# Plain float32 products in place of three float32r products on split operands

## What is computed

```python
h = rmsnorm(x, ln_mix_g)
proj = h @ w_in                                   # split into dq, dk, dv, nq, ..., ng, mg
y_diff = diff_attention(dq, dk, dv, lam, ...)
y_nsa = nsa_attention(nq, k_cmp, v_cmp, k_slc, v_slc, k_win, v_win, sigmoid(ng))
mixed = merge0 * (y_diff @ w_proj_diff) + merge1 * (y_nsa @ w_proj_nsa)
x = x + mixed @ w_out
x = x + square(relu(rmsnorm(x, ln_mlp_g) @ w_mlp_up)) @ w_mlp_down
q, k, v, f_logit, gate = split(rmsnorm(x, norm_a_g_2) @ w_in_a_2)
x = x + (fox_attention(q, k, v, log_sigmoid(f_logit + b)) * silu(gate)) @ w_out_a_2
k, v = split(rmsnorm(x, kv_norm_g_2) @ w_kv_2)
q, gate = split(rmsnorm(x, norm_b_g_2) @ w_in_b_2)
x = x + (swa_sink_attention(q, k, v, sinks) * silu(gate)) @ w_out_b_2
```

## Time and profile before

| | |
|---|---|
| median of 3 runs | 2090.55 us |
| lowest, highest | 2073.0, 2091.24 us |
| span of the profiled execution, first to last instruction | 2072.2 us |
| PE busy | 1907.3 us (92%), 8846 matmuls |
| DVE, ACT, POOL busy | 908.2, 717.1, 368.5 us |
| granted TensorE clock, mean | 0.920 |

### The profile page before, as it was taken

One profiled execution on the slowest core, in us unless ns is written; L12 is line 12 of the kernel. 1 busy time (PEld: TensorE's weight loads), 2 busy tenths in 40 slices (PEclk: granted clock), 3 DMA queues, 4 the chain that ended last, 5 costly groups with the idle time before them and its releaser, 6 DMA issues.

```text
span 2072.2 us, 24116 instructions
## 1 busy us (share of the span) xinstructions
PE 1907.3 (92%) x8846; PEld 1443.5 (70%) x8846; DVE 908.2 (44%) x1569; ACT 717.1 (35%) x1525; POOL 368.5 (18%) x490
## 2 busy tenths in 40 slices
PE   3999898999979999898999999989999998798988
PEld 2888567877755655687788888777775556686647
DVE  2583364225534555334443243234623443453662
ACT  3223365122144555423342142233223442333550
POOL 4240132102114444111000000000102330020330
PEclk9999797999977999999899999989996878898889
DMA  5223121332101221322222332312221102132212
GB/s 138 73 91 127 46 66 56 102 102 81 41 24 38 52 51 40 123 95 93 72 87 101 102 102 83 101 63 80 89 85 46 47 21 82 61 102 65 52 26 81
DMA packets 148050, 154.85 MB, mean 75 GB/s; under 512 B 48973, under 2 KB 90173, under 8 KB 147961
## 3 DMA queue, kind: packets, MB, share of 16 engines
q1 hardware_dynamic: 141768, 152.74, 23.2%
q0 software_dynamic: 992, 0.86, 0.3%
q10 hardware_dynamic: 5200, 0.02, 0.3%
HBM read 123.15 MB, written 2.15 MB: 60 GB/s over the span
## 4 chain that ended last, share of the span: by engine, by line
PE 90%; DVE 4%; ACT 3%; ACTq 1%; issue 1%; POOL 0%; DVEq 0%; POOLq 0%
PE ps L1421 58%; PE ps L1650 11%; PE ps L1677 5%; PE ps L1697 4%; PE ps L1711 3%; PE ps L1658 2%; ACTq L476 1%; PE ps L1654 1%; PE ps L1692 1%; DVE qkt L1008 1%; PE ps L1549 1%; PE ps L1519 1%; PE ps L1620 1%; ACT qkt L633 1%; PE ps L1537 1%
## 5 line engine op out<-in xcount | busy, mean ns | idle before, releaser
L1421 PE MATMUL ps<-spl,ht 128*128 128x512 f32 x2496 | 581.3, 395 | 31.0 <-DVE spl L787 15.8
L1421 PEld LDWEIGHTS ps<-spl,ht 128*128 128x128 f32 x2496 | 476.5, 191 | 135.3 <-issue 14.8
L787 DVE TENSOR_TENSOR spl<-raw,spl 128x1024 fp32r<-128x1024 f32 x196 | 253.4, 1336 | 566.2 <-ACT spl L494 566.2
L494 ACT ACTIVATE spl<-raw 128x1024 fp32r<-128x1024 f32 x196 | 196.2, 1052 | 637.3 <-PE ps L1421 636.5
L1421 PE MATMUL ps<-ht,spl 128*128 128x512 f32 x1536 | 349.9, 390 | 2.0 <-DVE spl L787 2.0
L1421 PEld LDWEIGHTS ps<-ht,spl 128*128 128x128 f32 x1536 | 288.5, 188 | 62.7 <-issue 2.9
L1650 PE MATMUL ps<-qkt 64*128 64x256 f32 (+2 forms) x960 | 255.4, 378 | 11.3 <-issue 5.8
L978 DVE TENSOR_REDUCE nm<-ps 128x1 f32<-128x512 f32 (+5 forms) x320 | 150.7, 471 | 146.8 <-PE ps L1658 144.0
L614 ACT ACTIVATE pb<-ps,nm 128x512 f32<-128x512 f32 (+5 forms) x320 | 162.1, 511 | 119.0 <-DVE nm L978 118.7
L1650 PEld LDWEIGHTS ps<-qkt 64*128 64x128 f32 x960 | 160.5, 212 | 61.0 <-issue 42.6
L1421 PE MATMUL ps<-spl,uu 128*128 128x512 f32 x768 | 174.4, 389 | 0.0
(11 more groups left out here) (244 smaller groups left out, 1547.3 us busy)
## 6 DMA issues: line engine op xcount, KB each, us to landing
raw<-w_in SPq DMA_DIRECT2D x30, 1024.0 KB, 5.2
raw<-w_mlp_up SPq DMA_DIRECT2D x16, 1024.0 KB, 5.2
raw<-w_mlp_down SPq DMA_DIRECT2D x16, 1024.0 KB, 5.0
raw<-w_in_a SPq DMA_DIRECT2D x16, 1024.0 KB, 5.3
stq<-qkv SPq DMA_DIRECT2D x56, 256.0 KB, 2.7
raw<-w_in_b SPq DMA_DIRECT2D x8, 1024.0 KB, 4.9
stq<-qkv SPq DMA_DIRECT2D x48, 128.0 KB, 2.5
raw<-w_proj_diff SPq DMA_DIRECT2D x4, 1024.0 KB, 5.2
```

Source lines behind the costliest of these rows:

```text
L494: act.activation(SPL[:, n % 2, HI, 2 * k:2 * k + 2], RAW[:, n % 2, 2 * k:2 * k + 2], ACT.Copy).then_inc(hi_done, 1)
L787: dve.tensor_tensor(SPL[:, n % 2, LO, 2 * k:2 * k + 2], RAW[:, n % 2, 2 * k:2 * k + 2], SPL[:, n % 2, HI, 2 * k:2 * k + 2].bitcast(F32), A ...
L1421: last = pe.matmul(PS[:, b0 + b], left[:, x], right[:, y], start=(kt == 0 and i == 0), stop=(kt == UK * g["units"] - 1 and i == 2))
```

## The change

Each product becomes one matmul on float32 operands, and no half is made. The weight is multiplied straight from RAW, which now has four slots; SP refills a slot when PE has used it. HT, UU and QKT hold float32 values once, YS is Y itself, and a second copy of HT with the other norm's gains (HTK) feeds the key and value projection of the banded attention. ACT evicts the even slices of a norm and DVE the odd ones. ACT copies the queries and DVE the keys. The scores of both maps of a tile stand next to each other, followed by both masks. The reload of X now waits until PE has used the last unit that reads Y.

```diff
-        RAW = region("raw", "raw", [2, UK, W])
-        SPL = region("spl", "spl", [2, 2, UK, W], F32R)
+        RAW = region("raw", "raw", [SLOTS, UK, W])
...
-                    if n >= 2:
-                        sp.wait_ge(lo_done, 2 * (n - 1))
+                    if n >= SLOTS:
+                        sp.wait_ge(unit_used, n - SLOTS + 1)
...
-            weights(RUNS["merge"], skip=2, only=4)
-            sp.wait_ge(y_hi, 2 * KT)
-            sp.wait_ge(y_lo, 2 * KT)
+            weights(RUNS["merge"], skip=2, only=8)
+            sp.wait_ge(unit_used, RUNS["merge"][4]["unit"])
             sp.dma_start(X[:], I["x"][0].rearrange("(t p) n -> p t n", p=P)).then_inc(x_in[0], 16)
-            weights(RUNS["merge"], skip=4)
+            weights(RUNS["merge"], skip=8)
...
-            def split_hi(n, hold=()):
...
-                for k in range(2):
-                    act.activation(SPL[:, n % 2, HI, 2 * k:2 * k + 2], RAW[:, n % 2, 2 * k:2 * k + 2],
-                                   ACT.Copy).then_inc(hi_done, 1)
...
-                for kt in range(KT):
+                for kt in range(KT) if k == 3 else range(0, KT, 2):
                     act.wait_ge(x_tr, KT * k + kt + 1)
-                    act.activation(HT[:, HI, kt], PS[:, bank_of(k, kt)], ACT.Copy,
-                                   scale=1.0 if k == 3 else LNG[:, k, kt:kt + 1]).then_inc(x_hi, 1)
+                    act.activation(HT[:, kt], PS[:, bank_of(k, kt)], ACT.Copy,
+                                   scale=LNG[:, 4 if k == 3 else k, kt:kt + 1]).then_inc(x_even, 1)
...
-                for i, (x, y) in enumerate(((HI, HI), (HI, LO), (LO, HI))):
-                    last = pe.matmul(PS[:, b0 + b], left[:, x], right[:, y], start=(kt == 0 and i == 0),
-                                     stop=(kt == UK * g["units"] - 1 and i == 2))
-                return last
+                w = RAW[:, (g["unit"] + u) % SLOTS, k]
+                left, right = (src[:, kt, cols], w) if g["kind"] == "tok" else (w[:, cols], src[:, kt])
+                return pe.matmul(PS[:, b0 + b], left, right, start=(kt == 0), stop=(kt == UK * g["units"] - 1))
...
-                        for i, (x, y) in enumerate(((HI, HI), (HI, LO), (LO, HI))):
-                            pe.matmul(bank[:, 0:w], QKT[r, m.slot, 0, x, P * t:P * t + P],
-                                      QKT[r, m.slot, 1, y, P * a.first_key(t):P * t + P],
-                                      start=(i == 0), stop=False, skip_group_check=True)
+                        pe.matmul(bank[:, 0:w], QKT[r, m.slot, 0, P * t:P * t + P],
+                                  QKT[r, m.slot, 1, P * a.first_key(t):P * t + P],
+                                  start=True, stop=False, skip_group_check=True)
+                    for h in range(2):
+                        bank = PS[:, 2 * (idx % 2) + h]
                         if a.is_fox:
```

## The result

The changed kernel takes 2186.99 us (2185.85 to 2188.04, 4 runs) against 2081.78 before (2071.62 to 2091.24, 4 runs): 1.05 times the time, 95% interval 1.0443 to 1.0557. The profiled execution has a span of 2185.8 us, 113.6 more than before, where the sum of the prediction had 191. The kernel before varies by some 20 us from run to run here, the changed one by 2 us.

The account below looks back on a forecast made before the run. PE's busy time was taken as the bound. From 2072.2 us: +309 weight products, +3 narrow gates, -80 scores, -56 waits gone, +15 new wait gave 2264; 9 for longer runs made 2273 us, range 2218 to 2362.

Parts of the forecast that it names:

- +309: Weight products: 1728 products at 0.859 us plain instead of 0.680 add 309 us (+299 to +346).
- The bound of 0.880: Weight products: upper bound in us per plain product, if each half carries the 13 ns a float32r matmul takes over 512 cycles.
- rival 4: Weight products: four passes at float32r's price, 0.907 us a product, giving 2356 us; 5%.
- The three norms: Between PE's last product before a norm and its next: 8 us instead of 17.6, -10 each, -30 together.
- The new wait for X: Before w_out: PE stands 12 us while X reloads ahead of w_out's first unit; with the clock's fall, +15 us.
- PE's start: Kernel start: PE needs four slices, two made by DVE, instead of waiting for eight LO slices and half a weight; -5 us.
- the scores' term: Attention scores: plain maps side by side and fewer copies save 106 us, three quarters kept, -80; bounds -106 and 0.
- the copies: Attention: one copy by ACT and one by DVE replace four dependent instructions; perhaps 8 of 15.9 us of waits go.
- Rival 2: Attention scores: the two maps don't overlap, a pair takes as long as before, time 2353 us; 7%.
- Rival 3: Attention: it falls to the low clock, time at most 2544 us; 6%.
- Rivals 1 and 5: Plain matmuls: 1, they cost what float32r ones do, 1572 us, 3%; 5, weight products at low clock, 3740 us, 3%.
- Rival 6: Waits, chiefly at norms: they don't shrink because DVE and ACT are late in their new order, 2329 us; 6%.

Follow-up runs that it names:

- e5: Kernel before with only the weight products plain: one float32 matmul on the HI halves for three float32r ones, LO halves unused; 2388.07 us.
- e4: Changed kernel with the reload of X behind the first two units of w_out on SP instead of ahead of them; 2177.37 us.
- e1: Kernel before with the changed kernel's attention alone: plain scores of both maps side by side, masks after, weights still three float32r matmuls; 1930.49 us.
- e3: Kernel before with the changed kernel's plain scores and single copies, but each map's mask directly behind its own scores, so maps are apart; 2083.91 us.
- e6: Changed kernel with each map's mask behind its own scores, so the two maps' products no longer stand next to each other; 2356.14 us.
- e9: Kernel before with only the masks moved: map 0's three float32r score matmuls, map 1's three, then both masks; 1957.43 us.
- e2: Kernel before with the three float32r score matmuls of the two maps alternating and both masks following; 1948.9 us.
- e7: Kernel before with one float32r score matmul (HI by HI) per map in place of three, maps still apart; 1973.96 us.
- e10: Kernel before with one float32r score matmul (HI by HI) per map in place of three, maps next to each other, masks behind them; 1919.64 us.

## Why the prediction was wrong

**Right.** PE's time per product decided, and the halves' removal was worth only the waits. A plain product took 858.4 ns for 859 forecast, the mean of one matmul 592 to 599 ns for "near 600"; at the measured rate the term is +308 for +309, and e5, with the narrow gates left as they were, is 314 us of span above the kernel before (293 above its median). The bound of 0.880 and the four-pass price of 0.907 (rival 4) are off. The Trainium skill's sentence of four passes ("FP8 and Floating Point Precision", on TensorE's precision notes) fits only as two matmuls at two cycles a column, without float32r's 13 ns per pass (858.4 ns are 2060 cycles of 2.4 GHz, 4.02 a column). The three norms take 6.2, 7.6 and 7.5 us where 17.6, 16.6 and 17.6 were, -31 for -30. The new wait for X was 10.5 us for 12, and e4 shows its cause as it was given; taken out it gave 9.6 back, where the sum had +15 for it. PE's start moved by 2.2 us (43.73 to 41.52) for 5. Everything outside the four attentions grew by 277 us, where these terms make 285.5: the stages of weights and norms were right to 9 us.

**The step that failed** is the scores' term: "Other engines take some of it back ... That leaves three quarters, -80 us". Attention and its entries gave 163 us where -80 and about 15 of the waits were written. The direction and the mechanism, two maps side by side on PE, were right; the size was off by 68 us. Three parts of it were wrong.

1. Nothing was taken back. NSA's unit went from 13.22 us (756.70 to 769.92 before) to 10.26 (731.92 to 742.18), or 10.34 over ten units. I had 2.2 us of saving per unit and discounted it to 1.7; it was 2.9. DVE, at 107.52 of 177 us, had room, as its 122.61 of 228 already said. No row gave the size of the quarter taken off, and it cost the sum 26 us.
2. The pair was priced a little high. Side by side the second mask adds next to nothing: 0.21 us for both against the 0.32 that I kept; and the 256-wide tile, taken as 0.39 less, went from 1.34 to 0.76 us in the unit that follows 731.92. The four pairs of a unit save 2.7 us for the 2.2 forecast.
3. The clock was held fixed. I divided the saving by the clocks of before, so that a slow FOX stayed slow at 0.72. In fact the time at the low clock fell from 204 to 66 us, and FOX rose from 0.72 to 0.86, NSA from 0.93 to 0.99. e1 and e3 show that this comes with the overlap (83 against 192 us with the same plain matmuls), e5 that the weights do not bring it, and the middle of FOX that the clock goes with the overlap in all seven traces named there.

How much falls to each can be estimated from a unit's length at full clock, taken from the start times of its scores:

| | unit before, us | unit now, us | units | saved by units, us | saved by the stretch, us |
|---|---|---|---|---|---|
| DIFF | 11.83 | 9.25 | 8 | 21 | 25 |
| NSA | 13.22 | 10.34 | 16 | 46 | 57 |
| FOX | 15.15 | 12.58 | 8 | 21 | 48 |
| SWA | 11.86 | 9.71 | 8 | 17 | 33 |

That is 105 us by shorter units, for the 84 forecast at full clock, and 58 us by the clock and by entries and ends, for some 37 (14 by the division by the clocks, 8 by the copies, 15 of the waits). So of the 68 us some 26 are the discount, 21 the units and 21 the rest, most of it in FOX, where the larger part of the saving is the clock's. It is an estimate: no run changed the clock alone.

The time of 2273 has 9 us more, for runs like the two longer ones of the kernel before; the changed kernel has no such run in four.

**The rivals.** Rival 2 (no overlap) was priced at 2353 us; e6 is that kernel and took 2356. That it is so close is in part luck: the 2353 hold the 9 us for longer runs, and the pair took 2.43 us, not the 2.09 of before. In spans it is 2343 against 2354.3. Even so, the sum's other terms hold together, and it was the overlap's worth, 168 us for the 80 that I gave it, which put the result out of range. Rival 3 foresaw that attention's clock would move, and had the direction wrong: "the same rows are at work in less time", said against it, fits what the middle of FOX shows. Rivals 1 and 5 did not occur. Rival 6 didn't either; the norms' waits shrank as forecast.

The range failed with the term: its lower bound gave the scores at most 106 us, as though -106 excluded any more, although the trace of before showed FOX at a clock of 0.72, and the earlier trace rows gave no reason why it should stay there. With -106 in the sum the forecast would have been 2247 us, still 60 above what was measured.

## What to carry to other kernels

Where two products use different halves of the array's rows, put them next to each other with no full-row matmul between; look at the start times of such pairs in the trace before anything else is done to them. Here the masks' place between two score maps was worth 156 us of span between e1 and e3, and 117 to 142 on the old halves (e9, against the span and against the run beside it), more than the number format of the scores did in either order (e3 is within the spread of the kernel before, e1 18 us below e2). When a change makes matmuls run side by side, price the clock as a term of its own, with the low-clock stretches of before as its bound, rather than dividing by the clock that was. Don't take a discount off a sum of rows without a row that shows who would take it back. And judge "one matmul for three" by what one of them takes: plain float32 was dearer by 26% here, so it paid only in attention, where it shortened a chain of copies.

## What the runs showed of the hardware

- A plain float32 matmul of 512 columns appears as two matmuls of 429.2 ns each (439.48 us for 1024), a float32r one as one of 226.7 ns (348.22 us for 1536).
- Matmuls on the row halves 0 to 63 and 64 to 127, into different banks, ran side by side in both formats, even with all of the first half's matmuls ahead of the second's in the program (e9: six of 512 columns in 0.90 us). The Trainium skill, "TensorEngine Tiling (Array Packing)", section on tiling modes, says that tiles operate independently; the traces agree, at 1.12 us a pair with its masks against 2.09.
- The granted clock in FOX followed the overlap, not PE's share of busy time: in the middle of the stage it was 0.79 to 0.91 with PE busy for all of it and the maps apart (before, e3, e6, e7), and 0.98 to 1.00 with PE busy for 94 to 99% and the maps side by side (the changed kernel, e9, e10).
- Kernels differ in how steady they are: the kernel before took 2073.46 to 2107.1 us beside the experiments, at a mean clock of 0.921 down to 0.902, while four runs of e1 lie within 4 us at 0.942 to 0.945.
- A long stage of plain products keeps the full clock. The changed kernel's MLP stage, with the columns of the earlier trace rows:

```profile
1031.00:1470.00 439.00, 439.00 (x1024) 194.32 (x1023) 31.43 (x45) 21.73 (x49) 0.00 (x0) 1.00 0.23 74
```
